# Three attentions on one core: the value product with the values stationary and two heads in two column halves, results feature-major, inverse row sums spread once per group

## What is computed

```python
# chunk attention
sc = jnp.einsum("bqhd,bkhd->bhqk", qc, kc) * scale + bias
p = jax.nn.softmax(sc, axis=-1)
return jnp.einsum("bhqk,bkhd->bqhd", p, vc)
...
# latent attention
s = (einsum('bqhd,bkhd->bhqk', qn, kn) + einsum('bqhr,bkr->bhqk', qr, kr)) * scale
pm = jax.nn.softmax(where(rel >= 0, s, NEG), axis=-1)
return jnp.einsum('bhqk,bkhd->bqhd', pm, v)
...
# sliding window, with a sink logit in the softmax
pm = jax.nn.softmax(jnp.concatenate([s, sink], axis=-1), axis=-1)[..., :-1]
o = jnp.einsum('bnhgqk,bnkhd->bqhgd', pm, vb)
...
# what follows: a product with the output weights; in the second block the result is gated first
y = (... + gates[:, :, 1] * ((ob * jax.nn.silu(b_z)) @ w_br_b)
         + gates[:, :, 2] * ((oc * jax.nn.silu(c_z)) @ w_br_c))
```

## Time and profile before

| what | value |
|---|---|
| time, median of 3 runs | 2645.8 us (2643.38 to 2648.6) |
| the profiled execution's own time | 2643.3 us |
| its span | 2641.5 us |
| its mean granted TensorE clock | 0.978 |
| PE busy, share of the span | 2521.2 us, 95% |
| DVE busy | 1447.6 us, 55% |
| ACT busy | 1112.0 us, 42% |
| chain that ended last | PE 88%, DVE 7%, ACT 2%, issue 2% |

### The profile page before, as it was taken

One profiled execution on the slowest core, in us unless ns is written; L12 is line 12 of the kernel. 1 busy time (PEld: TensorE's weight loads), 2 busy tenths in 40 slices (PEclk: granted clock), 3 DMA queues, 4 the chain that ended last, 5 costly groups with the idle time before them and its releaser, 6 DMA issues.

```text
span 2641.5 us, 32188 instructions
## 1 busy us (share of the span) xinstructions
PE 2521.2 (95%) x11846; PEld 2029.3 (77%) x11846; DVE 1447.6 (55%) x2381; ACT 1112.0 (42%) x1975; POOL 41.8 (2%) x28
## 2 busy tenths in 40 slices
PE   5998999999999999999999999999989999999998
PEld 2886788887777778888777777778867777777886
DVE  6778655556656553433446644554454664455445
ACT  4575433433535443443345433433443543333243
POOL 2000000000000000000000000000010000000001
PEclk8999999999999999999999999999999999999999
DMA  5435466565221123222222111212322121122233
GB/s 229 158 105 191 148 203 208 202 211 191 72 80 64 41 88 105 98 100 97 96 88 72 66 63 60 75 66 96 104 77 91 65 72 64 61 72 68 89 103 104
DMA packets 77901, 280.33 MB, mean 106 GB/s; under 512 B 8640, under 2 KB 8896, under 8 KB 77504
## 3 DMA queue, kind: packets, MB, share of 16 engines
q1 hardware_dynamic: 60624, 218.02, 24.4%
q10 hardware_dynamic: 17136, 60.37, 6.9%
HBM read 276.26 MB, written 2.10 MB: 105 GB/s over the span
## 4 chain that ended last, share of the span: by engine, by line
PE 88%; DVE 7%; ACT 2%; issue 2%; DMA 0%; ACTq 0%; SPq 0%; DVEq 0%
PE ps L220 25%; PE ps L222 24%; PE ps L221 24%; PE ps L1761 2%; PE ps L1675 1%; PE ps L1735 1%; PE ps L1578 1%; PE ps L1091 1%; PE ps L1679 1%; DVE wl L215 1%; PE ps L1635 1%; PE ps L486 1%; PE ps L1039 1%; PE ps L487 1%; ACT wh L212 1%
## 5 line engine op out<-in xcount | busy, mean ns | idle before, releaser
L215 DVE TENSOR_TENSOR wl<-raw,wh 128x1024 fp32r<-128x1024 f32 x374 | 459.2, 1228 | 701.8 <-ACT wh L212 700.6
L220 PE MATMUL ps<-xh,wl 128*128 128x512 f32 x1744 | 699.4, 401 | 20.9 <-DVE wl L215 11.2
L222 PE MATMUL ps<-xh,wh 128*128 128x512 f32 x1744 | 683.1, 392 | 0.0
L221 PE MATMUL ps<-xl,wh 128*128 128x512 f32 x1744 | 682.6, 391 | 0.0
L212 ACT ACTIVATE wh<-raw 128x1024 fp32r<-128x1024 f32 x374 | 395.0, 1056 | 683.1 <-PE ps L222 636.7
L220 PE MATMUL ps<-bh,wl 128*128 128x512 f32 x1158 | 460.5, 398 | 23.8 <-DVE bC L1522 7.2
L221 PE MATMUL ps<-bl,wh 128*128 128x512 f32 x1158 | 454.8, 393 | 0.0
L222 PE MATMUL ps<-bh,wh 128*128 128x512 f32 x1158 | 454.5, 392 | 0.0
L220 PEld LDWEIGHTS ps<-xh,wl 128*128 128x128 f32 x1744 | 329.1, 189 | 139.1 <-issue 49.5
L222 PEld LDWEIGHTS ps<-xh,wh 128*128 128x128 f32 x1744 | 329.3, 189 | 70.8
L221 PEld LDWEIGHTS ps<-xl,wh 128*128 128x128 f32 x1744 | 329.8, 189 | 66.0 <-issue 1.4
(11 more groups left out here) (306 smaller groups left out, 2607.3 us busy)
## 6 DMA issues: line engine op xcount, KB each, us to landing
raw<-in_w SPq DMA_DIRECT2D x388, 512.0 KB, 3.2
bA<-in_ada ACTq DMA_DIRECT2D x74, 512.0 KB, 4.5
bC<-in_ada SPq DMA_DIRECT2D x9, 512.0 KB, 10.6
bD<-in_ada ACTq DMA_DIRECT2D x8, 512.0 KB, 5.3
bS<-in_ada ACTq DMA_DIRECT2D x8, 512.0 KB, 4.9
bS<-in_attn_bias ACTq DMA_DIRECT2D x8, 512.0 KB, 3.2
bC<-in_ada ACTq DMA_DIRECT2D x6, 512.0 KB, 4.0
bD<-in_ada SPq DMA_DIRECT2D x5, 512.0 KB, 15.0
```

Source lines behind the costliest of these rows:

```text
L215: e.tensor_tensor(wl[p][:], raw[p][:], wh[p][:].bitcast(F32), ALU.subtract)\
L220: e.matmul(out, wl[p][:, blk, 0:M], xhi, start=start, stop=False)
L221: e.matmul(out, wh[p][:, blk, 0:M], xlo, start=False, stop=False)
L222: return e.matmul(out, wh[p][:, blk, 0:M], xhi, start=False, stop=stop)
```

## The change

`values` swaps the operands: 64 columns of values are the stationary operand, 128 columns of turned exponentials the moving one. Head 0 writes partitions 0 to 63 and head 1 partitions 64 to 127 of the same 128 columns, so the result is feature-major; the four steps of a group fill one bank, `ps[6 + t % 2]` for group t, and the loop over the heads is now the inner one. The row sums of a group stay in eight columns of `crow`; one reciprocal (`inverses`) makes the eight inverses. `spread` brings them to feature-major form: for each step and head a product of one column, broadcast to 64 stationary columns, with the identity. The transposes of the result are gone. In the A loop VectorE copies the bank of results (L1264 of the changed kernel) and multiplies the copy with the spread bank (L1266); in the low loop it multiplies the gate with the results (L1820) and then with the spread bank (L1823). The call moves from step 4t + 6, between turn and `unit_out`, to the end of step 4t + 5, after `values`. The sink terms of the sliding window are added for eight columns at once.

```diff
@@ pair_steps (A loop); low_pair has the same in values and inverses
                 def values(n):
                     st = steps[n]
                     if pe:
-                        if n >= 2:
-                            need(f"{s}{n - 2}o")
+                        if n >= 2 * NT and n % NT == 0:
+                            need(f"{s}{n // NT - 2}y")
                         need(f"{s}{n}pt1")
-                        for m in range(2):
-                            for b in range(st["nk"] // P):
+                        at = P * (n % NT)
+                        for b in range(st["nk"] // P):
+                            for m in range(2):
                                 x = pt(n, 0)[:, m * st["nk"]:(m + 1) * st["nk"]] if whole(n) else pt(n, m)
-                                mm = e.matmul(ps[6 + n % 2][:, HD * m:HD * m + HD], x[:, P * b:P * b + P], st["v"][m][b],
+                                mm = e.matmul(ps[6 + n // NT % 2][HD * m:HD * m + HD, at:at + P], st["v"][m][b], x[:, P * b:P * b + P],
                                               start=b == 0, stop=b == st["nk"] // P - 1)
                         done(mm, f"{s}{n}pv")
 
-                def results(n):
+                def inverses(t):
+
+                    c = 8 * (t % 2)
                     if dve:
-                        c = 2 * (n % 4)
-                        need(f"{s}{n}ex1")
-                        done(e.reciprocal(sm[:, SIN + c:SIN + c + 2], sm[:, SSM + c:SSM + c + 2]), f"{s}{n}ri")
-                        need(f"{s}{n}ri")
-                        need(f"{s}{n}pv")
-                        done(e.tensor_tensor(steps[n]["o"], ps[6 + n % 2][:, 0:P].rearrange("p (m d) -> p m d", m=2),
-                                             sm[:, SIN + c:SIN + c + 2].unsqueeze(2).to_broadcast([P, 2, HD]), ALU.mult), f"{s}{n}o")
+                        need(f"{s}{NT * t + NT - 1}ex1")
+                        if t >= 2:
+                            need(f"{s}{t - 2}spread")
+                        done(e.reciprocal(crow[:, RI + c:RI + c + 8], crow[:, RS + c:RS + c + 8]), f"{s}{t}ri")
 
+            def spread(s, t, bank):
+
+                need(f"{s}{t}ri")
+                for i in range(NT):
+                    for m in range(2):
+                        c = RI + 8 * (t % 2) + 2 * i + m
+                        mm = e.matmul(ps[bank][HD * m:HD * m + HD, P * i:P * i + P], crow[:, c:c + 1].to_broadcast([P, HD]), ident,
+                                      start=True, stop=True)
+                done(mm, f"{s}{t}spread")
...
-            def out_turn(j, bank):
+            def out_spread(j, bank):
 
                 if pe:
-                    need(f"A{4 * j + 3}o")
-                    for i in range(NT):
-                        mm = e.transpose(ps[bank][:, P * i:P * i + P], o_rows(j)[:, i, :], ident)
-                    done(mm, f"O{j}tt")
-                if act:
-                    need(f"O{j}tt")
-                    done(e.activation(bh[:, j, :], ps[bank][:], ACT.Copy), f"Ohi{j}")
+                    spread("A", j, bank)
+                if dve:
+                    need(f"A{4 * j + 3}pv")
+                    need(f"A{j}spread")
+                    done(e.tensor_copy(o_all(j), ps[6 + j % 2][:]), f"A{j}o")
+                    need(f"A{j}o")
+                    done(e.tensor_tensor(o_all(j), o_all(j), ps[bank][:], ALU.mult), f"A{j}y")
+                if act:
+                    need(f"A{j}y")
+                    done(e.activation(bh[:, j, :], o_all(j), ACT.Copy), f"Ohi{j}")
                 if dve:
                     need(f"Ohi{j}")
-                    done(e.tensor_tensor(bl[:, j, :], ps[bank][:], bh[:, j, :].bitcast(F32), ALU.subtract), f"Olo{j}")
+                    done(e.tensor_tensor(bl[:, j, :], o_all(j), bh[:, j, :].bitcast(F32), ALU.subtract), f"Olo{j}")
...
-                if i == 2 and n >= 6:
-                    out_turn((n - 6) // NT, 1)
+                if i == 1 and 5 <= n < N:
+                    out_spread((n - 5) // NT, 1)
...
@@ low loop
+            def gated_spread(s, t, p, z):
+
+                bank, used = grab()
+                if pe:
+                    e.wait_ge(s_bank[bank], used + 1)
+                    spread(p, t, bank)
+                if dve:
+                    need(f"{p}{NT * t + NT - 1}pv")
+                    done(e.scalar_tensor_tensor(z, ps[6 + t % 2][:], 0.5, z, ALU.mult, ALU.mult), f"{p}{t}y")
+                    need(f"{p}{t}y")
+                    need(f"{p}{t}spread")
+                    e.tensor_tensor(z, z, ps[bank][:], ALU.mult).then_inc(s_bank[bank], 1)
+                if act:
+                    e.wait_ge(s_bank[bank], used + 2)
+                    done(e.activation(bh[:, Z_AT[t], :], z, ACT.Copy), f"{s}hi{t % 4}")
+                gated_low(s, t % 4, z, Z_AT[t])
...
-                    if k % NT == 2 and k >= 6 and k < N:
-                        t = (k - 6) // NT
-                        gated_out(f"{n}Mb" if t < 4 else f"{n}Mc", t % 4, o_pair(t), lambda: need(f"{s}{4 * t + 3}o"), z_of(t),
-                                  4 + t if t < 4 else t - 4, 0.5)
                     for it in outs:
                         unit_out(it, 2)
...
                     if 0 <= k - 1 < N:
                         values(k - 1)
+                    if k % NT == 1 and 5 <= k < N:
+                        t = (k - 5) // NT
+                        gated_spread(f"{n}Mb" if t < 4 else f"{n}Mc", t, s, z_of(t))
```

More of the change, by code:

```diff
@@ L1270, in program @@
                     scale=[r_q(j, i, m) for m in range(2)], bias=[bS[:, 2 * (j % 2) + m, T - nk:T] for m in range(2)],
-                    v=[[v_tok(j)[:, b, HD * m:HD * m + HD] for b in range(i + 1)] for m in range(2)],
-                    o=o_rows(j)[:, i, :].rearrange("p (m d) -> p m d", m=2)))
-            scores, maximum, exponential, turn, turned, values, results = pair_steps(
+                    v=[[v_tok(j)[:, b, HD * m:HD * m + HD] for b in range(i + 1)] for m in range(2)]))
+            scores, maximum, exponential, turn, turned, values, inverses = pair_steps(
                 "A", steps, lambda n, m: bA[:, 2 * (n % 2) + m, :], lambda n, m: p_rows[2 * (n % 2) + m])
@@ L1762, in values, with inverses @@
+                        for b in range(st["nk"] // P):
+                            for m in range(2):
+                                x = pt(n, 0)[:, m * st["nk"]:(m + 1) * st["nk"]] if whole(n) else pt(n, m)
+                                mm = e.matmul(ps[6 + n // NT % 2][HD * m:HD * m + HD, at:at + P], st["v"][m][b], x[:, P * b:P * b + P],
                                               start=b == 0, stop=b == st["nk"] // P - 1)
                         done(mm, f"{s}{n}pv")
-                def results(n):
+                def inverses(t):
+                    c = 8 * (t % 2)
@@ L1777, in low_pair @@
-                return scores, maximum, exponentials, turn, turned, values, results
+                        need(f"{s}{NT * t + NT - 1}ex1")
+                        if steps[NT * t]["sink"]:
+                            need(f"{s}{NT * t + NT - 1}es")
+                            done(e.tensor_tensor(col(RS + c, 8), col(RS + c, 8), col(ES + c, 8), ALU.add), f"{s}{t}sk")
+                            need(f"{s}{t}sk")
+                        if t >= 2:
+                            need(f"{s}{t - 2}spread")
@@ L1780, in gated_turn @@
+                        done(e.reciprocal(col(RI + c, 8), col(RS + c, 8)), f"{s}{t}ri")
+                return scores, maximum, exponentials, turn, turned, values, inverses
             def gated_turn(s, t, rows_, ready, z, at, scale):
@@ L2111, in program @@
                         steps.append(dict(
-                            low=True, sink=None, nk=nk, o=o, scale=col(C_RQ + i), ready=low_ready if k == 0 else nothing, values=nothing,
+                            low=True, sink=None, nk=nk, scale=col(C_RQ + i), ready=low_ready if k == 0 else nothing, values=nothing,
                             q=[qn(t)[r[m], P * i:P * i + P] for m in range(2)], k=[kn(t)[r[m], 0:nk] for m in range(2)],
@@ L2129, in program @@
                             v=[[sw_v[:, b, r[m]] for b in range(k0 // P, i + 1)] for m in range(2)]))
-                scores, maximum, exponentials, turn, turned, values, results = low_pair(
+                scores, maximum, exponentials, turn, turned, values, inverses = low_pair(
                     s, steps, lambda k, m: bD[:, 4 + 2 * (k % 2) + m, :], lambda k, m: turned_rows[2 * (k % 2) + m])
```

50 lines of the change are left out of this document (19 added, 31 removed).

## The result

| | median | lowest to highest |
|---|---|---|
| before | 2644.96 us | 2643.38 to 2648.6 |
| changed | 2616.09 us | 2614.34 to 2616.69 |

The ratio is 0.9888 [0.9871, 0.9905]: 1.1% faster. The profiled execution took 2616.12 us, 27.2 less than that of before; the prediction had 34.6 less. The page of the changed kernel has this as busy time (to be set against the earlier trace rows): TensorE has 288 records more and is busy 18.7 us less.

What follows compares the result with a forecast made beforehand. The TensorE queue was taken as the bound. Terms of -30.7 (values), +11.6 (spread), +9.5 (A loop), -16.5 (waits) and -8.5 (clock) sum to -34.6 us; by the median before, the forecast is 2611, range 2598 to 2650.

Steps and rivals of the forecast that it cites:

- waits and clock: Low loops: 14 TensorE waits vanish with the new order, 16.5 us less, and five 1.2 GHz stretches with them, 8.5 less.
- Values and halves: Value products in A and low loops: the two column halves run side by side, 30.7 us less over 864 records.
- slot: Value products and spreads: a pair of records, one per column half, taking 0.11 us together; 624 in all.
- Staggered halves: Rival, value products and spreads: second half starts in the first's second pass, 13 us more, 2624; chance 0.12.
- the halves don't overlap: Rival, value products and spreads: records run one behind another, 0.11 us apart; +29 in all, 2675; chance 0.16.
- loads stand bare: Rival, value products and spreads: each slot costs 0.05 us more for its exposed weight load, 31 us, 2642; chance 0.06.
- DVE in the A loop: A loop: VectorE's group-end operations ahead of the 512-column maximum stall PE, 9.5 us more in all.
- late maximum: Low loops: the following step's maximum comes some 2 us late, covered by a PE unit of 5.5 us.
- The chain S to S + 5.0: A loop: from the next scores' start S, VectorE's copy through the second head's first operation ends at S + 5.0.
- its saving of 1.5 and 0.4 on top: A loop's last group: PE waits for DVE and ACT anyway, so a 1.5 us saving is lost, plus 0.4.
- waits stay: Rival: bank late in another step, or clock falls elsewhere, as at new A-loop stalls; 25 us not won, 2636; chance 0.12.
- three spreads: Spreads at the loops' ends, among full-array products: changes of shape and loads cost 0.8 us each, 2.4 more.

Runs made afterwards that it cites:

- one half: Changed kernel with heads outermost and both heads of a step written to the same column half, output rearranged; 2653.45 us, ratio 1.0033.
- place alone: Kernel before with only the low loop's gated_out call moved behind the unit's readout and the values of the same step; 2621.28 us, ratio 0.9906.
- the split: Changed kernel with the A loop's group end in three places: copy ahead of the next scores, lo behind the next maximum, product and hi staying; 2601.83 us, 0.9841.
- the old place: Changed kernel with the low loop's gated_spread back at step 4t + 6, between turn and unit_out; 2646.41 us, ratio 1.0006.
- copy's wait moved: Changed kernel whose A-loop copy of results waits for the values alone, the wait for the spread standing behind it; 2609.8 us, ratio 0.9856.

## Why the prediction came out as it did

**Direction and range: right.** The forecast was 2611, the time 2616. The profiled difference came out 7.4 us smaller than forecast: 3.5 of it in the A loop, 1.2 in the low loops' product and 3.1 outside the loops, less 0.4 that waits and clock gave more.

**Values and halves: right.** The steps have the predicted length to 0.01 us, and the kernel with one half confirms the price of a slot. Values and spread together gave 11.4 us in the windows of the low loops (place alone against the changed kernel) for 12.6 predicted (544 x 0.055 - 64 x 0.175 - 14 x 0.44; the last spread of each loop lies behind the window). Where the 1.2 went isn't traced. In the A loop a group without a stall is 17.16 - 16.06 = 1.1 us shorter than before; by the sum 40 x 0.055 - 4 x 0.175 - 0.44 = 1.06. "Staggered halves" and "the halves don't overlap" fell with this. So did "loads stand bare": a pair starts each 0.11 us, so neither half's load shows; the rule of the Trainium skill (TensorE: Matmul & The Clock Gate, Part 3, Packing small matmuls), that a load overlaps running matmuls only in another row group, is not what this trace shows.

**Waits and clock in the low loop: right, both terms.** The place alone gave 25.4 us for 16.5 + 8.5, in the two parts predicted: 16.5 of idle and 8.9 of busy time of PE. No stretch there is below 1.00. The late maximum was covered, as argued.

**The A loop: the mis-sized term.** It is "DVE in the A loop", 9.5 us, with a loop that "stays about as it is". Up to the last value the loop is 4.1 us longer, where the prediction's terms give 0.6 (-12.0 for values, +3.1 for seven spreads, +9.5); the term is worth about 13. The chain S to S + 5.0 was right (its parts add to 5.1): with S = 800.85 the first head began at 804.73 and the second at 805.93, S + 3.88 and S + 5.08. But the stall counts from where all four matmuls would run together, 1.37 us a group (17.43 - 16.06), not 1.1: 8.2 us in six groups for 6.6. The larger miss is in the last group, costed at its saving of 1.5 and 0.4 on top. From its last scores on, the loop takes 916.39 - 904.57 = 11.8 us against 911.37 - 901.83 = 9.5 before and 903.51 - 895.44 = 8.1 with the split: 3.8 us lost, not 1.9. Up to the start of the last turn it is 911.68 - 904.57 = 7.1 us against 900.82 - 895.44 = 5.4 with the split, 1.7 lost, about as costed: no large products lie there, so the four operations of VectorE pass to the maximum, ScalarE's readout and the turn. The other 2.0 are clock, which the sum left out here. While PE waits, the clock falls to 0.50 for 6.8 us, which before has nowhere near its last group, and the last turn and values take 4.71 us for 2.69:

```profile
908.85 0.74 DVE L1052 SCALAR_TENSOR_TENSOR bA<-ps,crow,bS 128x512 f32<-128x512 f32 x1
...
910.35 0.72 ACT L1060 ACTIVATE bA<-bA,sm 128x512 f32<-128x512 f32 x1 [0.19 <-DVE sm L1054]
...
911.07 0.47 ACT L1083 ACTIVATE bD<-ps 128x384 f32<-128x384 f32 x1
...
911.68 1.94 PE L1070 MATMUL ps<-cst,bA 128*128 128x128 f32 x8 [4.27 <-ACT bD L1083]
```

```profile
910.70:917.50 6.80, 5.82 (x38) 5.09 (x39) 0.20 (x1) 2.04 (x5) 0.00 (x0) 0.50 0.01 2
```

That is the part of the rival "waits stay" that came true: the clock fell at a new wait of the A loop. And a condition that the prediction took as given, that the copy starts only when the spread is done (S + 0.07), was worth 5.6 us by itself and could be dropped.

**Outside the loops: 5.5 us for 2.4.** The prediction has three spreads there, at 0.8 each. The largest part, 3.0 us, lies between the A loop and the first low loop (593.16 us for 590.19). About 1.0 of it is the new code: kernels with the changed A loop whose clock stood as long at 0.50 there as in before, 17 us in all, took 591.1 to 591.2. The other 2.0 are clock. "Place alone" shows it with the very instructions of before: it took 592.63, with 24 us at 0.50. The 7 us more lie in two spots, behind 1319 and behind 1465; each pair of rows is before and then "place alone":

```profile
1326.10:1329.40 3.30, 3.30 (x16) 2.69 (x16) 3.30 (x6) 1.84 (x3) 0.00 (x0) 1.00 0.00 0
```

```profile
1325.20:1328.60 3.40, 3.40 (x9) 2.63 (x8) 3.40 (x7) 1.85 (x3) 0.00 (x0) 0.50 0.00 0
```

```profile
1465.00:1472.70 7.70, 6.27 (x29) 5.46 (x30) 3.90 (x11) 4.18 (x12) 0.00 (x0) 0.78 0.21 68
```

```profile
1465.00:1472.70 7.70, 6.28 (x28) 5.44 (x28) 3.19 (x10) 3.76 (x12) 0.00 (x0) 0.56 0.19 68
```

All thirteen profiles sort this way: four with 17 us at 0.50 took 590.2 to 591.2, one with 21 took 591.8, six with 24 or 25 took 592.6 to 593.8, one with 27 took 594.0 and one with 32 took 595.6. The profile of before has as little as any, so some 2 us of the 7.4 that are missing are luck of the execution; what decides the number of such stretches stays open.

## What to carry to other kernels

Two independent products of 64 stationary columns cost as much here as one (0.11 us for either) if they sit in the two column halves and the program alternates between them. Look at least as hard at what else a rewrite moves: the order in two other engines' queues gave 22 us by itself, without the new product, and the new product and spread with the old place gave nothing; together they gave 29. A needless wait on a semaphore in the rewritten part took 6 us back. When a stall is priced, measure step lengths from start to start, since the waits list leaves out what the first half of a pair hides. Before a difference of 2 to 5 us is put down to an edit, look at stretches whose instructions are the same in both kernels.

## What was not expected of the hardware

- A matmul for a free column half overtook three others in program order and no more (of eight and eight, five ran first, then the halves alternated); 7 us of 2616 hang on it.
- In a wait of PE of 4.3 us the clock fell to 1.2 GHz and stayed there for 6.8 us; one of 4.0 (copy's wait moved) was followed by 3.4 us of it, those of 1.9, 2.7 and 2.9 at the same place in the other kernels by none, though waits of 1.6 us in the low loop of before were followed by 3.4 us of it.
- Identical instructions between the loops took 590.2 us in one execution and 592.6 in another. The clock stood at 1.2 GHz for 17 us in the one and for 24 in the other.
